# A two-block transformer stack on one core: order of VectorE's sums in the squared-ReLU stages, order of ScalarE's copies in the first attention, and the engine of the squares in the second

## The reference, cut to what matters

```python
def first_block(x, c, positions, ...):
    for i in range(DEPTH):                       # 2 layers
        mod = jax.nn.silu(c) @ ada_w[i] + ada_b[i]
        sh_a, sc_a, g_a, sh_f, sc_f, g_f = jnp.split(mod[:, None, :], 6, axis=-1)
        h = rms_norm(x, attn_norm[i]) * (1.0 + sc_a) + sh_a
        y = sparse_mixer(h, ...) if i % 2 == 0 else diff_mixer(h, ...)
        x = x + g_a * y
        h = rms_norm(x, ffn_norm[i]) * (1.0 + sc_f) + sh_f
        x = x + g_f * swiglu(h, ffn_w_gate[i], ffn_w_up[i], ffn_w_down[i])   # 1024 -> 2816 -> 1024

# in diff_mixer, for 8 heads of 128 columns:
        p = masked_softmax(s, key_idx[None, :] <= pos[:, None])
        a = p[:, :, 0] - lam * p[:, :, 1]
        o = jnp.einsum('bhqk,bhkd->bhqd', a.astype(v.dtype), v)
    o = rms_norm(o, out_norm) * (1.0 - lam_init)

# in second_block (layer 0: pool mixer, on x and on a context; layer 1: attention):
        h_lat = h_lat + g2 * sq_relu_mlp(m_l, mlp_w1[i], mlp_w2[i])          # 1024 -> 4096 -> 1024
        h_ctx = h_ctx + cg2 * sq_relu_mlp(m_c, mlp_w1[i], mlp_w2[i])         # layer 0 alone

def sq_relu_mlp(h, w1, w2):
    return jnp.square(jax.nn.relu(h @ w1)) @ w2
```

## Time and profile before

| what | value |
|---|---|
| device time, median of 3 runs | 1620.73 us (1617.89 to 1621.85) |
| profiled execution | span 1622.4 us (no other time is listed for it) |
| TensorE busy | 1523.8 us (94%), 8949 matmuls |
| VectorE busy | 1023.7 us (63%), 1599 instructions |
| ScalarE busy | 762.4 us (47%), 1184 instructions |
| transfers | 335.28 MB, mean 207 GB/s |

### The profile page before, as it was taken

The page is one execution under the profiler, slowest core; times in us unless marked ns, Lnnn a source line. Parts: engine busy times, 40 slices in busy tenths (PEclk is TensorE's granted clock), DMA queues, the critical chain, the costliest instruction groups (busy, mean ns, idle before and its releaser), DMA issues.

```text
span 1622.4 us, 21897 instructions
## 1 busy us (share of the span) xinstructions
PE 1523.8 (94%) x8949; PEld 1216.8 (75%) x8949; DVE 1023.7 (63%) x1599; ACT 762.4 (47%) x1184; POOL 0.2 (0%) x4
## 2 busy tenths in 40 slices
PE   5989799999999799999999999899999988999997
PEld 3767777888787567787878878688787766778786
DVE  3566755666668866565585655766557684466655
ACT  3344553344544354333455554555545534355543
POOL 0000000000000000000000000000000000000000
PEclk9999999999999899999999999999999999999999
DMA  9992158756466658876748555566554754245452
GB/s 364 339 325 105 53 182 315 251 187 234 156 235 207 208 183 293 308 254 211 269 157 283 180 177 203 183 234 207 176 188 149 267 181 156 78 130 182 168 197 90
DMA packets 167908, 335.28 MB, mean 207 GB/s; under 512 B 8184, under 2 KB 109184, under 8 KB 167808
## 3 DMA queue, kind: packets, MB, share of 16 engines
q1 hardware_dynamic: 140992, 235.09, 42.7%
q10 hardware_dynamic: 26816, 98.79, 16.7%
HBM read 332.81 MB, written 1.05 MB: 206 GB/s over the span
## 4 chain that ended last, share of the span: by engine, by line
PE 60%; DVE 25%; ACT 8%; issue 4%; DMA 2%; ACTq 0%; SPq 0%; DVEq 0%
PE ps L1780 11%; PE ps L1781 11%; PE ps L1782 11%; PE ps L1849 11%; DVE wlo L1072 9%; PE ps L1850 5%; ACT whi L620 4%; DVE hbuf L1094 3%; PE ps L1726 3%; ACT hbuf L640 2%; DMA ring<-in_ada_w_dram 1%; DVE res L1162 1%; DVE work L1160 1%; PE ps L2023 1%; DVE hT L1217 1%
## 5 line engine op out<-in xcount | busy, mean ns | idle before, releaser
L1072 DVE TENSOR_TENSOR wlo<-wraw,whi 128x1024 fp32r<-128x1024 f32 (+1 forms) x420 | 493.2, 1216 | 277.2 <-ACT whi L620 276.8
L620 ACT ACTIVATE whi<-wraw 128x1024 fp32r<-128x1024 f32 (+1 forms) x420 | 419.1, 1046 | 261.1 <-PE ps L1782 137.5
L1849 PE MATMUL ps<-hT,whi 128*128 128x512 f32 x1472 | 526.7, 401 | 1.6 <-DVE hT L1217 1.5
L1850 PE MATMUL ps<-hT,wlo 128*128 128x256 f32 x1472 | 413.5, 281 | 0.0
L1849 PEld LDWEIGHTS ps<-hT,whi 128*128 128x128 f32 x1472 | 277.4, 188 | 81.5 <-issue 9.1
L1850 PEld LDWEIGHTS ps<-hT,wlo 128*128 128x128 f32 x1472 | 279.1, 190 | 0.0
L1780 PE MATMUL ps<-whi,act_hi 128*128 128x512 f32 x560 | 220.1, 393 | 9.1 <-DVE wlo L1072 9.1
L1781 PE MATMUL ps<-wlo,act_hi 128*128 128x512 f32 x560 | 218.3, 390 | 0.0
L1782 PE MATMUL ps<-whi,act_lo 128*128 128x512 f32 x560 | 218.2, 390 | 0.0
L1780 PE MATMUL ps<-whi,hT 128*128 128x512 f32 (+2 forms) x416 | 161.1, 387 | 6.3 <-DVE hT L1217 5.7
L1781 PE MATMUL ps<-wlo,hT 128*128 128x512 f32 (+2 forms) x416 | 157.8, 379 | 0.0
(11 more groups left out here) (223 smaller groups left out, 1344.3 us busy)
## 6 DMA issues: line engine op xcount, KB each, us to landing
wraw<-in_mlp_w_dram SPq DMA_DIRECT2D x96, 1024.0 KB, 5.2
ring<-in_ada_w_dram ACTq DMA_DIRECT2D x80, 1024.0 KB, 6.7
wraw<-in_ffn_w_gate_dram SPq DMA_DIRECT2D x22, 1024.0 KB, 5.3
wraw<-in_ffn_w_up_dram SPq DMA_DIRECT2D x22, 1024.0 KB, 7.1
wraw<-in_ffn_w_down_dram SPq DMA_DIRECT2D x22, 1024.0 KB, 4.9
work<-in_ada_w_dram ACTq DMA_DIRECT2D x12, 1024.0 KB, 11.9
wraw<-in_diff_w_in_dram SPq DMA_DIRECT2D x12, 1024.0 KB, 5.1
wraw<-in_attn_w_qkv_dram SPq DMA_DIRECT2D x12, 1024.0 KB, 5.6
```

Of the source, the lines that this page charges most:

```text
L620: nc.scalar.activation(whi[:, u % 2, part], raw_view(u)[:, part], ACT.Copy).then_inc(hi_ready, 1)
L1072: nc.vector.tensor_tensor(wlo[:, u % 2, part], raw_view(u)[:, part], whi[:, u % 2, part].bitcast(F32), ALU.subtract).then_inc(lo_ready, 1)
L1849: mm(ps[:, bank, :], whi[:, u % 2, c0:c0 + P], hT[:, :, k, :], start=(k == 0), stop=False, skip_group_check=True)
L1850: ins = mm(ps[:, bank, 0:S], wlo[:, u % 2, c0:c0 + P], hT_hi[:, k, :], start=False, stop=(k == KT - 1), skip_group_check=True)
```

## The change

Three edits; the arithmetic stays.

- Squared-ReLU stages: in VectorE's `stream`, kind "up" calls `hidden_out(i)` before `split_unit(i + 2)`; kind "pair" keeps its order. The condition for the split is written in another way. ScalarE's `stream` is not touched.
- First attention (stage 0): in ScalarE's loop `copy_pt(i - 1)` comes before `exps(i)`.
- Second attention (stage 1): VectorE's multiplication and reduction for the head norm are taken out; ScalarE gets `squares`, two Square activations of 128 columns with an accumulated sum per step, two steps after the copy that it follows, and one more call behind the loop. It waits for `a.taken`; a new semaphore counts the squares, and VectorE waits for all eight ahead of the head norm.

```diff
 # ScalarE, attention(stage)
+                def squares(i):
+                    act.wait_ge(a.taken, i + 1)
+                    if i >= 2:
+                        act.wait_ge(sem("a1_squares"), i - 1)
+                    for t in range(TT):
+                        ins = nc.scalar.activation(hbuf[:, i % 2, t * P:(t + 1) * P], r1[:, t, i * P:(i + 1) * P], ACT.Square,
+                                                   accum_out=stat[:, TT * i + t:TT * i + t + 1])
+                    ins.then_inc(sem("a1_squares"), 1)
+
                 for i in range(a.steps + a.lag + 1):
+                    if stage == 0 and a.lag <= i < a.steps + a.lag:
+                        copy_pt(i - a.lag)
                     if i < a.steps:
                         exps(i)
-                    if a.lag <= i < a.steps + a.lag:
+                    if stage != 0 and a.lag <= i < a.steps + a.lag:
                         copy_pt(i - a.lag)
+                    if stage == 1 and i > a.lag + 1:
+                        squares(i - a.lag - 2)
                     if i < a.ada:
                         ada_step()
...
+                if stage == 1:
+                    squares(a.steps - 1)
 # VectorE, stream
                 for i in range(s_["count"]):
-                    if i < s_["count"] - 2:
+                    if s_["kind"] == "up":
+                        hidden_out(s_, i)
+                    if i < s_["count"] - 1 or not hold_last:
                         split_unit(s_["base"] + i + 2)
-                    if i == s_["count"] - 2 or i == s_["count"] - 1 and not hold_last:
-                        split_unit(s_["base"] + i + 2)
-                    hidden_out(s_, i)
+                    if s_["kind"] == "pair":
+                        hidden_out(s_, i)
 # VectorE, take(i), stage 1
                         nc.vector.tensor_copy(o, ps[:, 6, 0:256].rearrange("p (t d) -> p t d", t=TT)).then_inc(a.taken, 1)
-                        dve.wait_ge(a.taken, i + 1)
-                        o2 = hbuf[:, i % 2, 0:2 * P].rearrange("p (t d) -> p t d", t=TT)
-                        link(nc.vector.tensor_tensor(o2, o, o, ALU.mult))
-                        link(nc.vector.tensor_reduce(stat[:, TT * i:TT * i + TT], o2, AX, ALU.add))
 # VectorE, behind attention(1)
+            dve.wait_ge(sem("a1_squares"), ATT[1].steps)
             link(nc.vector.tensor_scalar(stat[:, 0:n], stat[:, 0:n], 1.0 / HD2, EPS, ALU.mult, ALU.add))
```

More of the change, by code:

```diff
@@ L1079, in hidden_out @@
             def hidden_out(s_, i):
-                if s_["kind"] == "down":
-                    return
                 u = s_["base"] + i
```

## The result

The changed kernel took 1600.0 us (median of 4 runs, 1595.32 to 1604.31) against 1621.29 us (1617.89 to 1628.93): a ratio of 0.9848, with a 95% interval of 0.981 to 0.9885, or 24.6 us (18.6 to 30.8). Run again with other kernels, it gave 0.9856 (0.9832 to 0.988), 23.4 us. The forecast was 20.8.

A forecast was written before the change was run, and what follows sets the result against it. TensorE was busy 94% of the span, so only its standstills and late instructions could give time back. Terms of 14.4, 2.5 and 3.9 made 20.8 us, from 1620.7 to 1599.9, so 1600 us, range 1592 to 1610.

The forecast's parts named there:

- Sums ahead of the low split: Squared-ReLU stages: the sum runs while the low split would wait for ScalarE, saving 14.4 us, bounds 10.9 to 16.2.
- late units: First two squared-ReLU stages: eight units in each go from 5.82 to 5.55 us, 4.3 us saved.
- the stops: Down stages: TensorE's nine waits for VectorE's low split before a unit's first product, 9.1 us, would go.
- slow first products: Down units: the product after each of nine waits takes 0.50 against 0.39 us; 1.0 us would go.
- the third stage's pace: Third squared-ReLU stage: 5.55 us per unit would add 1.8 us, counted only in the upper bound.
- Copies ahead of exponentials: First attention: transposes wait for the exponentials alone, saving 2.5 us, bounds -1.8 to 5.2.
- Squares on ScalarE: Second attention: VectorE's step falls from 4.23 to 3.32 us; 3.9 us saved in all, bounds 2.1 to 6.4.
- (first): Down stages: waits for the low split stay because four splits in sequence are too slow; 1610 us, chance 0.06.
- (second): Second attention: squares of 2.7 us make ScalarE the bound, 7.2 us lost; 1611 us, chance 0.04.
- (third): Whole kernel: nothing arrives, what is won is waited for later at residuals and norms; 1620 us, chance 0.04.
- (fourth): Both attentions: TensorE falls to its lower clock, 32 us lost; 1638 us, chance 0.03.
- the ring: Squared-ReLU stages: chain of waits through ScalarE and VectorE without TensorE, 5.81 us per unit, overtaking TensorE half-way.

## Why the prediction was right, point by point

- **Sums ahead of the low split (14.4 forecast, 10.9 to 16.2).** The mechanism is the forecast one. By time the size is 17.5 us (14.8 to 20.3). By stretches, against the one profile of the kernel before, it is 18.3 where all three stages ran at 5.55 us per unit, 16.6 to 16.7 in four executions where one ran at 5.65, and 14.0 to 14.2 in three where two did: from inside the range to 2 us above it. The late units are right: 2.0 us in each of the first two stages and 0.2 in the last unit of each, 4.4 for 4.3. The mis-sized term is the stops, 10.1 in the forecast. The lengths of the last up unit and the first three down units, before less after, are 4.5, 4.1 and 3.5, together 12.1; less the 0.4 of the last up units 11.7 remain. I took the idle time in front of the product, but a product lasts 0.39 us and the next begins 0.23 us after it. In front of the earlier trace rows's stop the last one is

```profile
948.46 0.39 PE L1782 MATMUL ps<-whi,act_lo 128*128 128x512 f32 x1
```

and the stop costs 950.05 - 948.46 - 0.23 = 1.36 us, 0.15 more than the idle time shown; over the nine stops it is 10.6 where the idle time is 9.1. The slow first products behind them add the 1.0 that the forecast had. The 1.5 us of the third stage's pace, 5.65 to 5.55, which I had only in a bound, is not the change's: the changed kernel, run again, had 5.65 there.
- **Copies ahead of exponentials (2.5, from -1.8 to 5.2).** 2.4 us in the loop. It does not always arrive, since TensorE's half-clock stretches lie otherwise: two of the changed kernel (us, busy us of PE, PEld, DVE, ACT, POOL, PEclk, DMA share, GB/s), where the earlier trace rows had one,

```profile
189.30:196.10 6.80, 5.67 (x33) 4.07 (x34) 3.77 (x9) 2.39 (x4) 0.00 (x0) 0.50 0.01 2
226.80:230.30 3.50, 3.50 (x14) 3.00 (x13) 1.08 (x3) 1.80 (x4) 0.00 (x0) 0.51 0.00 0
```

The loop and the stretch behind it took 92.0 to 97.1 us in nine executions with copies first (mean 94.2), 94.7 to 96.5 in four without (mean 95.5). That the edit pays in time is not shown.
- **Squares on ScalarE (3.9, 2.1 to 6.4).** 5.5 by time. The forecast was split at VectorE's last mixing (L1318, now L1333): it was to start 3.3 us earlier, and the tail behind it to save 0.6. In the kernel before, from the first maxima to the scaling of the sums:

```profile
525.10 0.42 DVE L1308 TENSOR_REDUCE rowmax<-ps 128x2 f32<-128x256 f32 x1 [1.31 <-PE ps L2008]
...
551.34 0.42 DVE L1308 TENSOR_REDUCE rowmax<-ps 128x2 f32<-128x256 f32 x1
...
555.57 0.18 DVE L1318 RECIPROCAL coef<-rowsum 128x4 f32<-128x4 f32 x1
...
557.43 0.90 PE L2023 MATMUL ps<-cst,work 128*128 128x128 f32 x3 [1.32 <-DVE work L1324]
...
562.02 0.42 DVE L1363 COPY work<-ps 128x256 f32<-128x256 f32 x1 [0.96 <-PE ps L2044]
...
563.40 0.17 DVE L1601 TENSOR_SCALAR stat<-stat 128x16 f32<-128x16 f32 x1
```

In the changed one, whose first maxima (517.74) and scaling (550.24) stand above:

```profile
544.24 0.17 DVE L1333 RECIPROCAL coef<-rowsum 128x4 f32<-128x4 f32 x1
...
546.09 0.55 PE L2035 MATMUL ps<-cst,work 128*128 128x128 f32 x3 [0.71 <-DVE work L1339]
...
548.98 0.42 DVE L1378 COPY work<-ps 128x256 f32<-128x256 f32 x1 [1.09 <-PE ps L2056]
```

From the first maxima the last mixing comes after 26.50 instead of 30.47 us, 4.0 for 3.3; the loop varies, though: first to last maxima took 26.2 to 26.3 us in three executions with the squares on VectorE and 22.7 to 24.9 in nine on ScalarE. From the last mixing to the scaling it is 6.00 instead of 7.83 us, 1.8 for 0.6. There TensorE's clock is what the forecast lacked: from the last transposes to the last taking (L1363, now L1378) the same instructions took 4.59 us before and 2.89 after, 1.7 of the 1.8. The granted clock from the last maxima to the scaling, in the kernel before and in the changed one (us, busy us of PE, PEld, DVE, ACT, POOL, PEclk, DMA share, GB/s):

```profile
551.30:563.40 12.10, 7.63 (x54) 5.47 (x56) 9.42 (x29) 3.09 (x11) 0.00 (x0) 0.66 0.40 138
```

```profile
541.00:550.20 9.20, 6.52 (x65) 4.68 (x69) 5.98 (x20) 6.88 (x36) 0.00 (x0) 1.00 0.68 228
```

All three executions with the squares on VectorE have a stretch of 10 us at half clock that begins in the tail; none of the nine with plain squares on ScalarE has one there. I had put the tail at full clock in both. Why the longer tail falls to half clock and the shorter does not is not shown beyond this.
- **Rivals.** The stops did not stay (first). ScalarE did not become the bound (second): its pair takes 0.6 to 0.7 us, where the rival had 2.7, against VectorE's 0.91. The Trainium skill ("ScalarE: Activation LUTs", "Rules for kernel authors") gives its factor of up to about three for bf16; the rival carried it over to fp32, and these fp32 rows don't bear that out. No run here has bf16. The parts arrive at the end and add up within their intervals (third). TensorE did not fall to its lower level in the attentions as a whole (fourth): stretches of 3.4 us in the first one stand in four of nine executions with the new order and in one of four with the old.
- **The sum.** 20.8 forecast; 24.6 and 23.4 by the ratios, with 20.8 inside both intervals. Too small were the stops (by 1.6) and the third part (by 0.7 up to the last mixing and 1.2 behind it); the copies' term was too large by about 1, as far as the means of 94.2 and 95.5 tell. TensorE's pace alone moves the first part by up to 4 us between executions, so how near the sum comes is in part luck.

## What to carry to other kernels

Where two engines hand a buffer round, look for work that is ready when the unit ends but stands in program order behind work that must first wait for the other engine: moving it forward cut the ring here and cost nothing that a trace shows. Price a stop by the distance of starts less the regular distance, not by the idle time shown, and price a moved instruction in the loop and in the tail apart: six of the eight pairs of squares run behind the last maxima, and there their time counts when they are made three times. Before two profiles are subtracted, compare a point ahead of the first edit; here 6.4 of 28.9 us lay there.

## What the runs showed of the hardware that was not expected

In the squared-ReLU stages TensorE has two paces for the same up unit without any wait shown, 5.55 and 5.65 us (the product with the high split lasts 391 to 395 ns in the median at the one, 398 at the other), and keeps one for a whole stage, unless the ring overtakes it. In thirteen profiled executions the first squared-ReLU stage had 5.65 in four, the second in one, the third in nine (the late units aside), and the changed kernel, profiled twice, had both in its third. It is worth 1.5 us a stage; what chooses it stays open. And the time ahead of the first attention varies from execution to execution by 10 us (128 to 138 us from TensorE's first product to the first score) with the same instructions. Between the changed kernel's two profiled executions, 8.1 us apart, it makes 5.1 us.
